# Delta heads: the next head's decays move from the solver to the scan, one difference and one weight split ahead of the masks, the taps behind the residuals

## Chip, core and metric

One core of a Trainium2 chip runs the whole kernel. The metric is the device time of one execution in microseconds; several executions are timed and their median is taken. The timed executions of the kernel before are 2096.05, 2089.41 and 2095.82.

## What is computed

One transformer block in fp32 (`D_MODEL` 1024, 512 tokens and 256 context tokens): a gated FFN, a mixer (grouped attention beside a gated delta rule in both directions), and a second FFN. The change touches only the delta rule, 8 heads of width 128. Cut to what matters:

```python
def _delta_rule(q, k, v, beta, g, s0):          # per head, in chunks
    gcum = jnp.cumsum(gc, axis=-1)
    decay = jnp.exp(jnp.where(lower_incl, gcum[..., :, None] - gcum[..., None, :], -jnp.inf))
    kb = kc * bc[..., None]
    l_mat = jnp.where(strict, jnp.einsum('nbhid,nbhjd->nbhij', kb, kc) * decay, 0.0)
    rhs = jnp.concatenate([vc * bc[..., None], kb * jnp.exp(gcum)[..., None]], axis=-1)
    sol = lax.linalg.triangular_solve(l_mat, rhs, left_side=True, lower=True, unit_diagonal=True)
    u, w = sol[..., :dv], sol[..., dv:]
    intra = jnp.where(lower_incl, jnp.einsum('nbhid,nbhjd->nbhij', qc, kc) * decay, 0.0)
    def step(s, xs):
        v_new = u_c - jnp.einsum('bhcd,bhde->bhce', w_c, s)
        o = jnp.einsum('bhcd,bhde->bhce', q_d, s) + jnp.einsum('bhij,bhje->bhie', a_c, v_new)
        s = s * d_c[..., None, None] + jnp.einsum('bhcd,bhce->bhde', k_d, v_new)
```

q, k and v of a head come from a GEMM, a convolution of three taps, silu, and (q, k) an l2 norm. The kernel uses chunks of 128 tokens, `NCH` = 6 of them, which gives the same result.

## The kernel before, in words

Each engine runs its own program (blocks `scalar` with `a`, `vector` with `v`, `gpsimd` with `g`, `tensor` with `pe`, `sync` with `sp`), in the order written out by hand, and semaphores join them: `then_inc` on an instruction, `wait_ge` ahead of one. An engine works in order, so what is queued behind a waiting instruction waits too.

**Weights.** The weights come in blocks of 128x1024. SP loads a block into the ring `raw`; `split(b)` on ScalarE rounds it into `w_hi` (L411), `split(b)` on VectorE subtracts (`w_lo`, L812, a tensor operation on two SBUF tensors), and the GEMM of the block waits for `w_split`. `step(b)` on VectorE is the split of the block two further on. A head has four blocks: 0 to 3 are q, k, v and the output gate z; `Blk(B_DN, h, 4)` to `(h, 6)` are those of the next head.

**A delta head** (`dn_head`, a loop over heads 0 to 6, and head 7 written out as the final one) has these parts on TensorE: sums of squares, GEMM of block 3, products k k and k q, transposes, three zero matmuls, the GEMM of the next head's block 4 (in all but the final head), transposes into `ps` (L1668), the **solver**, a **scan** over 6 chunks, and the rest of the next head's GEMMs, of which pieces (`fill`) lie in the scan.

**The solver** inverts a triangular matrix by levels: 18 steps `i`, three groups in each of six levels. In a step VectorE masks (`masked(i)`, L1226, reads PSUM and a mask in SBUF), TensorE multiplies (`mid(i)`, then `grow(i-1)`), ScalarE copies (L721). GpSimd makes each level's `d_s` (L370), and between them `d_qd` (L381), `d_kd` (L388) and `d_l` (L393). All of GpSimd's products here are tensor operations on two SBUF tensors.

**The scan** has for each chunk `t`: TensorE `from_keys(t)`, VectorE `residual(t)` (two of L1264), TensorE `solve(t)`, ScalarE `d_vn` (two of L730), TensorE `to_state(t)`, VectorE `new_state(t)` (two of L1274, at t = 0 of L1272).

**The decays.** For both directions d, VectorE takes the difference of cumulated gates (`decay_diff`, L1182, from the row table `g_row` that a GpSimd-issued DMA loads) into `d_q[:, 1]`, clips it (`decay_min`, L1187, into `d_t`), and makes the max with a mask (`decay_max`, L1190, into `d_r`). ScalarE exponentiates (`decay` L661, `decay_out` L665). `d_t[:, 0]` is multiplied by beta on VectorE, `d_t[:, 1]` on GpSimd (L363). In the kernel before these are made for the next head inside the solver, between masks.

On VectorE the order around the change is: norms of q and k, `step(b[2])`, products that lead to `d_l`, the off-mask products (L1218, L1221), `attn_mul` twice (L1232), `tables_next` (a copy of `hn`, L1153), the 18 masks with `step(b[3])` and the decays between them, three masks L1253, `step` of block 4, and the scan with one convolution tap (L1171, L1174) in each of the first three chunks.

Of the kernel before, what the change touches and what calls it, by code (L numbers as in the profile page):

```python
# [23 lines left out]
P = 128  # L24
# [5 lines left out]
NCH = NC_CTX + NC_X  # L30
# [55 lines left out]
def build(nc, W, WMOD, XT, VEC, CONV, CA, CB, OUT, XS, GR):  # L86
    ctx = ExitStack()
    with ctx:
# [316 lines left out]
        def _(a):  # L405
# [251 lines left out]
                split(b.ahead(2))  # L657

            def decay(h, d):
                a.wait_ge(s("d_mn"), h * 4 + (2 * d + 1))  # L660
                a.activation(d_t[:, d], d_t[:, d], ACT.Exp).then_inc(s("d_e1"), 1)  # L661

            def decay_out(h, d):
                a.wait_ge(s("d_mn"), h * 4 + (2 * d + 2))
                a.activation(d_r[:, d, 0:NC_X], d_r[:, d, 0:NC_X], ACT.Exp, scale=-1.0).then_inc(s("d_e2"), 1)  # L665

            def activate(h, ahead):
# [13 lines left out]
            def dn_head(h, final):  # L681
                b = [Blk(B_DN, h, j) for j in range(4)]
                take(b[2])
                a.wait_ge(s("d_ss"), h + 1)
                a.activation(d_rs[:, 0:SEQ], ps[:, 4, :], ACT.Ln, bias=eps_q, scale=float(DH))
                a.activation(d_rs[:, SEQ:SEQ + CTX], ps[:, 5, 0:CTX], ACT.Ln, bias=eps)
                a.activation(d_rs[:, SEQ + CTX:], ps[:, 6, :], ACT.Ln, bias=eps).then_inc(s("d_ln"), 1)
                a.wait_ge(s("d_ln"), h * 2 + 1)
                a.activation(d_rs[:], d_rs[:], ACT.Exp, scale=-0.5).then_inc(s("d_rstd"), 1)
                split(b[2].ahead(2))  # L690
                a.wait_ge(s("d_row"), h * 16 + 16)
                for d in range(2):
                    a.activation(d_qd[:, d], g_row[:, d, NC_CTX:], ACT.Exp).then_inc(s("d_qe"), 1)  # L693
                a.preload_act_table_set(SILU_SET)  # L694
                a.wait_ge(s("conv"), h * 3 + 3)
                a.activation(d_c[:, 2, :], d_c[:, 2, :], ACT.Silu).then_inc(s("d_silu"), 1)  # L696
                a.wait_ge(s("gemm_done"), b[3].n + 1)
                a.activation(d_z[:], bank(b[3], 1), ACT.Silu).then_inc(psum_read[b[3].pair], 1)
                a.preload_act_table_set(LOG_SET)  # L699

                a.wait_ge(s("d_tok"), h * 2 + 1)
                a.activation(d_ktok[:, 0:3].rearrange("p c n -> p (c n)"), ps[:, 2, 0:384], ACT.Copy)
                a.activation(d_ktok[:, 3:6].rearrange("p c n -> p (c n)"), ps[:, 7, 0:384], ACT.Copy).then_inc(s("d_tokc"), 1)
                split(b[3].ahead(2))
                a.wait_ge(s("d_tok"), h * 2 + 2)
                a.activation(d_vtok[:].rearrange("p (b c) n -> p b (c n)", b=2), ps[:, 0:2, 0:384], ACT.Copy).then_inc(s("d_tokc"), 1)
                a.wait_ge(s("t_open"), h + 1)
                for gr in range(3):
                    a.wait_ge(s("t_set"), h * 3 + gr + 1)
                    a.activation(ps[:, TRB[gr], 0:2 * P], d_q[:, 1, 2 * gr:2 * gr + 2].rearrange("p c n -> p (c n)"),  # L710
                                 ACT.Copy).then_inc(s("t_ps"), 1)
                if not final:
                    take_first(Blk(B_DN, h, 4))
                def scaled(c):
                    x = a.activation(d_l[:, 1, c], d_vtok[:, c], ACT.Identity, scale=hc[:, G_BETA + 6 + c:G_BETA + 7 + c])
                    if c == NCH - 1:
                        x.then_inc(s("d_vb"), 1)
                a.wait_ge(s("d_tokc"), h * 2 + 2)
                for i in range(18):
                    a.wait_ge(s("sv_q"), h * 18 + (i + 1))  # L720
                    a.activation(d_q[:, 0, 2 * (i % 3):2 * (i % 3) + 2].rearrange("p c n -> p (c n)"), ps[:, 2 + i % 2, 0:2 * P],  # L721
                                 ACT.Copy).then_inc(s("sv_qc"), 1)
                    if i < NCH:
                        scaled(i)
                    if not final and i in (6, 7, 12, 13):
                        (decay if i % 2 == 0 else decay_out)(h + 1, (i - 6) // 6)
                for t in range(NCH):
                    for d in range(2):
                        a.wait_ge(s("sc_t"), h * 12 + 2 * t + d + 1)
                        a.activation(d_vn[:, d, t % 2], ps[:, 4 + d, P:2 * P], ACT.Copy, scale=-1.0 if t else 1.0).then_inc(s("sc_n"), 1)  # L730
                if not final:
                    take(Blk(B_DN, h, 5))
                a.wait_ge(s("od_copy"), h + 1)
                a.activation(d_os[:], d_o[:], ACT.Square).then_inc(s("od_sq"), 1)
                if final:
                    round_attention(0, 6)
                    step(Blk(B_MERGE, 0, 0))
                else:
                    activate(h + 1, Blk(B_DN, h, 7))
                a.wait_ge(s("od_ss"), h + 1)  # L740
                a.activation(d_os[:], ps[:, 7, :], ACT.Ln, bias=eps, scale=1.0 / DH).then_inc(s("d_ln"), 1)
                a.wait_ge(s("d_ln"), h * 2 + 2)
                a.activation(d_os[:], d_os[:], ACT.Exp, scale=-0.5).then_inc(s("od_rstd"), 1)
# [3 lines left out]
            a.activation(d_up[:, CTX + 3:T + 3], bank(first[0], 1), ACT.Copy).then_inc(psum_read[first[0].pair], 1)  # L747
            split(first[0].ahead(2))
            for d in range(2):
                decay(0, d)  # L750
                decay_out(0, d)
            take(first[1])
            activate(0, first[1].ahead(2))
            with a.Fori(0, H - 1, 1) as h:
# [53 lines left out]
        def _(v):  # L808
# [368 lines left out]
            def decay_diff(h, d):  # L1177
                if d == 0:
                    v.wait_ge(s("d_row"), h * 16 + 16)
                else:  # L1180
                    v.wait_ge(s("d_mn"), h * 4 + 2)
                v.tensor_tensor(d_q[:, 1], hn[:, G_GC + 6 * d:G_GC + 6 * d + 6].unsqueeze(2).to_broadcast([P, NCH, P]),  # L1182
                                g_row[:, d], ALU.subtract).then_inc(s("d_diff"), 1)

            def decay_min(h, d):
                v.wait_ge(s("d_diff"), h * 2 + (d + 1))
                v.tensor_scalar(d_t[:, d], d_q[:, 1], 0.0, None, ALU.min).then_inc(s("d_mn"), 1)  # L1187

            def decay_max(d):
                v.scalar_tensor_tensor(d_r[:, d, 0:NC_X], d_q[:, 1, NC_CTX:], 0.0,  # L1190
                                       no_tri[:, d, :].unsqueeze(1).to_broadcast([P, NC_X, P]), ALU.max, ALU.add)\
                 .then_inc(s("d_mn"), 1)

            def dn_head(h, final):
                b = [Blk(B_DN, h, j) for j in range(4)]
# [2 lines left out]
                v.tensor_tensor(d_c[:, 1, 0:CTX], d_c[:, 1, 0:CTX], d_rs[:, SEQ:SEQ + CTX], ALU.mult)  # L1198
                v.tensor_tensor(d_c[:, 1, CTX + 2:], d_c[:, 1, CTX + 2:], d_rs[:, SEQ + CTX:], ALU.mult).then_inc(s("d_qk"), 1)
                v.tensor_tensor(d_c[:, 0, CTX + 2:], d_c[:, 0, CTX + 2:], d_rs[:, 0:SEQ], ALU.mult).then_inc(s("d_qk"), 1)  # L1200
                step(b[2])
                v.wait_ge(s("d_e1"), h * 2 + 1)
                v.tensor_tensor(d_t[:, 0], d_t[:, 0], bc(hc[:, G_BETA:G_BETA + 6]), ALU.mult).then_inc(s("d_eb0"), 1)

# [7 lines left out]
                v.tensor_tensor(d_l[:, 0].rearrange("p (b c) n -> p b (c n)", b=2),  # L1212
                                d_t[:, 0].rearrange("p (b c) n -> p b (c n)", b=2), ps[:, 4:6, 0:384], ALU.mult)\
                 .then_inc(s("d_l"), 1)
                v.wait_ge(s("d_l"), h + 1)
                for gr in range(3):
                    x = d_q[:, 1, 2 * gr:2 * gr + 2]
# [18 lines left out]
                attn_mul(1)  # L1236
                if not final:
                    tables_next(h + 1)
                for i in range(18):
                    masked(i)  # L1240
                    if i == 7:
                        step(b[3])
                    if final:
                        continue
                    if i in (2, 9):
                        decay_diff(h + 1, i // 9)
                    if i in (4, 11):
                        decay_min(h + 1, i // 11)
                    if i in (5, 12):
                        decay_max(i // 12)  # L1250
                for gr in range(3):
                    v.wait_ge(s("sv_t"), h * 21 + 18 + gr + 1)
                    v.tensor_tensor(d_w[:, gr].rearrange("p (d c) n -> p d c n", d=2),  # L1253
# [2 lines left out]
                if not final:  # L1256
                    v.wait_ge(psum_read[Blk(B_DN, h, 4).pair], Blk(B_DN, h, 4).turn + 2)
                    step(Blk(B_DN, h, 4))
                    v.wait_ge(s("d_qd"), h * 2 + 2)
                def residual(t):  # L1260
                    for d in range(2):
                        c = ORDER[d][t]
# [14 lines left out]
                for t in range(NCH):  # L1277
                    if t:
                        residual(t)
                    if t < NCH - 1:  # L1280
                        new_state(t)
                    if t < 3 and not final:
                        conv_tap(h + 1, 0, t)
                if not final:
                    v.wait_ge(s("sc_v"), h * 10 + 10)
                    tables(h + 1)
# [17 lines left out]
            step(Blk(B_DN, 0, 0))  # L1304
            for d in range(2):
                decay_diff(0, d)
                decay_min(0, d)
                decay_max(d)
            conv(0, 0, Blk(B_DN, 0, 0))
            conv(0, 1, Blk(B_DN, 0, 1))  # L1310
            step(Blk(B_DN, 0, 1))
# [589 lines left out]
```

## Time and profile before

| what | value |
|---|---|
| median of the three runs | 2095.82 us |
| the profiled execution | 2089.0 us |
| its span in the profile | 2087.3 us |
| TensorE busy | 2005.8 us (96%) |
| VectorE / ScalarE / GpSimd busy | 1126.4 / 797.7 / 225.4 us |
| mean granted TensorE clock | 0.985 of full speed |
| one delta head (transposes of head 0 at 913.36, of head 6 at 1353.79) | 73.4 us |

A row of the timeline has: start in us from the span's start, duration in us, engine, line and operation, output and inputs with their shapes, the count of merged instructions, and in brackets the idle time of the engine before it and what ended it.
### The profile page before, as it was taken

The numbers are of one execution on the slowest core, as the hardware profiler recorded it, in microseconds if no ns is written. First come the engines' busy times: TensorE is split into PE (matmuls) and PEld (weight loads), VectorE is DVE, ScalarE is ACT, GpSimd is POOL, SyncE is SP. The second block draws the span as 40 slices with busy tenths as digits, with TensorE's granted clock in tenths as the row PEclk, the third lists the DMA queues.
The fourth block names the chain that finished last, engine by engine and source line by source line (L and its number), as shares of the span: only waits on it lengthen the run. The fifth ranks groups of instructions, "written<-read, shape, count | busy, mean of one in ns | idle before, by whom it ended". The sixth has DMA issues, their size and how long they took to land.

```text
span 2087.3 us, 31229 instructions
## 1 busy us (share of the span) xinstructions
PE 2005.8 (96%) x11329; PEld 1714.1 (82%) x11329; DVE 1126.4 (54%) x2027; ACT 797.7 (38%) x1291; POOL 225.4 (11%) x211
## 2 busy tenths in 40 slices
PE   8999999999996999999999999999999979999996
PEld 4788888888884779888988888898888858888885
DVE  2677655555456655476676667666533353233335
ACT  4322222111236555465456536544422352223122
POOL 0000000000000210041342144133000000000000
PEclk9999999999998999999999999999999999999998
DMA  8233333333221330011011001100222413222322
GB/s 310 88 119 118 119 123 122 128 121 123 79 81 68 116 92 1 11 46 46 30 45 45 33 33 45 45 29 22 71 98 93 141 40 102 100 97 95 101 91 80
DMA packets 49035, 174.73 MB, mean 84 GB/s; under 512 B 6724, under 2 KB 6852, under 8 KB 48720
## 3 DMA queue, kind: packets, MB, share of 16 engines
q1 hardware_dynamic: 37632, 129.95, 18.4%
q0 software_dynamic: 11344, 43.97, 6.3%
q8 instruction: 40, 0.66, 0.1%
q14 instruction: 19, 0.16, 0.0%
HBM read 167.03 MB, written 4.24 MB: 82 GB/s over the span
## 4 chain that ended last, share of the span: by engine, by line
PE 86%; issue 5%; ACT 4%; DVE 4%; POOL 1%; DMA 0%; ACTq 0%; DVEq 0%; SPq 0%; POOLq 0%
PE ps L1370 79%; PE ps L1374 4%; PE ps L1608 1%; DVE d_w L1226 1%; ACT w_hi L411 1%; DVE X L894 1%; DVE n_y L886 1%; PE ps L1737 1%; POOL d_s L370 1%; DVE w_lo L812 0%; ACT L699 0%; ACT L694 0%; ACT d_qd L693 0%; ACT d_c L696 0%; DMA X<-XT 0%
## 5 line engine op out<-in xcount | busy, mean ns | idle before, releaser
L1370 PE MATMUL ps<-h_hi,w_hi 128*128 128x512 f32 (+1 forms) x1712 | 547.4, 369 | 16.7 <-DVE h_lo L869 10.9
L411 ACT ACTIVATE w_hi<-raw 128x1024 fp32r<-128x1024 f32 x221 | 233.8, 1058 | 794.5 <-PE ps L1370 794.5
L1370 PE MATMUL ps<-h_lo,w_hi 128*128 128x512 f32 (+1 forms) x1712 | 536.3, 360 | 0.0
L1370 PE MATMUL ps<-h_hi,w_lo 128*128 128x512 f32 (+1 forms) x1712 | 528.6, 358 | 0.0
L812 DVE TENSOR_TENSOR w_lo<-raw,w_hi 128x1024 fp32r<-128x1024 f32 x221 | 272.2, 1232 | 437.8 <-ACT w_hi L411 437.6
L1370 PEld LDWEIGHTS ps<-h_hi,w_hi 128*128 128x128 f32 x1712 | 318.8, 189 | 72.5 <-issue 22.9
L1370 PEld LDWEIGHTS ps<-h_lo,w_hi 128*128 128x128 f32 x1712 | 323.4, 189 | 49.1 <-issue 3.4
L1370 PEld LDWEIGHTS ps<-h_hi,w_lo 128*128 128x128 f32 x1712 | 323.6, 189 | 48.5
L1370 PE MATMUL ps<-g_hi,w_hi 128*128 128x512 f32 (+1 forms) x528 | 158.4, 355 | 0.0
L1370 PE MATMUL ps<-g_lo,w_hi 128*128 128x512 f32 (+1 forms) x528 | 157.9, 354 | 0.0
L1370 PE MATMUL ps<-g_hi,w_lo 128*128 128x512 f32 (+1 forms) x528 | 157.9, 354 | 0.0
L1226 DVE TENSOR_TENSOR d_w<-ps,cb 128x512 f32<-128x512 f32 x144 | 97.0, 686 | 64.9 <-PE ps L1374 44.4
L928 DVE TENSOR_TENSOR gt<-sg,ps 128x256 f32<-128x256 f32 (+1 forms) x66 | 37.5, 596 | 136.6 <-PE ps L1370 136.6
L1370 PEld LDWEIGHTS ps<-g_hi,w_lo 128*128 128x128 f32 x528 | 99.3, 188 | 14.1
L1370 PEld LDWEIGHTS ps<-g_lo,w_hi 128*128 128x128 f32 x528 | 99.3, 188 | 14.0
L1374 PE MATMUL ps<-d_q,d_w 128*128 128x128 f32 x576 | 110.1, 280 | 0.2
L1370 PEld LDWEIGHTS ps<-g_hi,w_hi 128*128 128x128 f32 x528 | 98.9, 188 | 13.8
L370 POOL TENSOR_TENSOR d_s<-d_l,cb 128x768 f32<-128x768 f32 x48 | 92.0, 1922 | 121.8 <-DVE d_q L1221 83.7
L1370 PE MATMUL ps<-d_w,d_s 128*128 128x128 f32 x576 | 92.9, 286 | 8.3 <-DVE d_w L1226 6.7
L721 ACT ACTIVATE d_q<-ps 128x256 f32<-128x256 f32 x144 | 55.2, 383 | 108.9 <-PE ps L1370 108.8
L1374 PE MATMUL ps<-d_w,d_q 128*128 128x128 f32 x480 | 93.8, 278 | 0.0
L831 DVE SCALAR_TENSOR_TENSOR m_part<-w_mod,silc,m_part 128x128 f32<-128x128 f32 x336 | 90.4, 343 | 0.0
(264 smaller groups left out, 2687.3 us busy)
## 6 DMA issues: line engine op xcount, KB each, us to landing
raw<-W SPq DMA_DIRECT2D x221, 512.0 KB, 3.4
w_mod<-WMOD POOLq DMA_DIRECT2D x56, 512.0 KB, 3.7
w_mod<-WMOD SPq DMA_DIRECT2D x16, 512.0 KB, 14.2
g_row<-g_rows POOLq DMA_DIRECT2D x8, 768.0 KB, 6.2
X<-XT SPq DMA_DIRECT2D x4, 768.0 KB, 7.4
a_sw<-i_n POOLq DMA_DIRECT2D x40, 64.0 KB, 1.9
x_spill<-X POOLq DMA_DIRECT2D x1, 2048.0 KB, 7.7
X<-x_spill POOLq DMA_DIRECT2D x1, 2048.0 KB, 8.4
```

Source lines behind the costliest of these rows:

```text
L370: g.tensor_tensor(d_s[lv % 2][:], d_l[:, 0], off_mask[:, lv, :].unsqueeze(1).to_broadcast([P, NCH, P]), ALU.mult).then_inc(s("lvl"), 1)
L411: a.activation(w_hi[:, b.pair], raw[:, b.raw], ACT.Copy).then_inc(s("w_hi"), 1)
L721: a.activation(d_q[:, 0, 2 * (i % 3):2 * (i % 3) + 2].rearrange("p c n -> p (c n)"), ps[:, 2 + i % 2, 0:2 * P], ACT.Copy).then_inc(s("sv_q ...
L812: v.tensor_tensor(w_lo[:, b.pair], raw[:, b.raw], w_hi[:, b.pair].bitcast(F32), ALU.subtract)\
L831: x = v.scalar_tensor_tensor(acc, w_mod[:, slot, k, :], silc[:, k, c:c + 1], acc, ALU.mult, ALU.add)
L886: v.tensor_tensor(n_y[:, k % 4, lo:T], cols(Y, Y2, p, k, lo, T), n_rs[:, lo:T], ALU.mult).then_inc(s("yn"), 1)
L894: last = v.scalar_tensor_tensor(x, n_y[:, k % 4, l:h_], drv[:, 2 * p + 1, k, sg_:sg_ + 1], x, ALU.mult, ALU.add)
L928: last = v.tensor_tensor(gt[:, l:h_], sg[:, l:h_], bank(blk, sg_), ALU.mult)
L1226: v.tensor_tensor(d_w[:, gr], ps[:, TRB[gr], :].rearrange("p (c n) -> p c n", c=4), tri_mask[:, lv - 1, :].unsqueeze(1).to_broadcast([P, 4 ...
L1370: return pe.matmul(out, lhsT, rhs, start=start, stop=stop)
L1374: return pe.matmul(out, lhsT, rhs, start=False, stop=True, skip_group_check=True)
L1608: last = pe.transpose(ps[:, c // 3, P * (c % 3):P * (c % 3) + P], a_p[:, i % 2, P * c:P * c + P], ident)
```

## The change

Six things move, nothing is added or left out of the computation:

- the differences are written into `d_t`, no more into `d_q[:, 1]`, and the clip works in place behind the max (`decay_clip`), with a wait between the two;
- difference 0 of the next head goes from behind mask 2 to ahead of mask 0, difference 1 from behind mask 9 to behind mask 2;
- the clips and maxes go from the solver to the scan: direction 0 ahead of `new_state(0)`, direction 1 behind `residual(1)`; ScalarE's exponentials go to the chunks 1 to 4 of the scan;
- `step(b[3])` goes from behind mask 7 to ahead of mask 0 (in the final head too);
- `step(b[2])` goes behind the product `d_l`;
- the taps go from behind `new_state` of chunks 0 to 2 to behind `residual` of chunks 2 to 4.

```diff
@@ scalar @@
             def decay(h, d):
+                a.wait_ge(s("d_mn"), h * 4 + (2 * d + 2))
+                a.activation(d_t[:, d], d_t[:, d], ACT.Exp).then_inc(s("d_e1"), 1)
+
+            def decay_out(h, d):
                 a.wait_ge(s("d_mn"), h * 4 + (2 * d + 1))
-                a.activation(d_t[:, d], d_t[:, d], ACT.Exp).then_inc(s("d_e1"), 1)
-
-            def decay_out(h, d):
-                a.wait_ge(s("d_mn"), h * 4 + (2 * d + 2))
                 a.activation(d_r[:, d, 0:NC_X], d_r[:, d, 0:NC_X], ACT.Exp, scale=-1.0).then_inc(s("d_e2"), 1)
...
-                    if not final and i in (6, 7, 12, 13):
-                        (decay if i % 2 == 0 else decay_out)(h + 1, (i - 6) // 6)
                 for t in range(NCH):
...
+                    if not final and t in (1, 2, 3, 4):
+                        (decay if t % 2 else decay_out)(h + 1, (t - 1) // 2)
@@ vector @@
             def decay_diff(h, d):
                 if d == 0:
                     v.wait_ge(s("d_row"), h * 16 + 16)
-                else:
-                    v.wait_ge(s("d_mn"), h * 4 + 2)
-                v.tensor_tensor(d_q[:, 1], hn[:, G_GC + 6 * d:G_GC + 6 * d + 6].unsqueeze(2).to_broadcast([P, NCH, P]),
+                v.tensor_tensor(d_t[:, d], hn[:, G_GC + 6 * d:G_GC + 6 * d + 6].unsqueeze(2).to_broadcast([P, NCH, P]),
                                 g_row[:, d], ALU.subtract).then_inc(s("d_diff"), 1)
 
-            def decay_min(h, d):
+            def decay_clip(h, d):
                 v.wait_ge(s("d_diff"), h * 2 + (d + 1))
-                v.tensor_scalar(d_t[:, d], d_q[:, 1], 0.0, None, ALU.min).then_inc(s("d_mn"), 1)
-
-            def decay_max(d):
-                v.scalar_tensor_tensor(d_r[:, d, 0:NC_X], d_q[:, 1, NC_CTX:], 0.0,
+                v.scalar_tensor_tensor(d_r[:, d, 0:NC_X], d_t[:, d, NC_CTX:], 0.0,
                                        no_tri[:, d, :].unsqueeze(1).to_broadcast([P, NC_X, P]), ALU.max, ALU.add)\
                  .then_inc(s("d_mn"), 1)
+                v.wait_ge(s("d_mn"), h * 4 + (2 * d + 1))
+                v.tensor_scalar(d_t[:, d], d_t[:, d], 0.0, None, ALU.min).then_inc(s("d_mn"), 1)
...
-                step(b[2])
                 v.wait_ge(s("d_e1"), h * 2 + 1)
...
+                step(b[2])
                 v.wait_ge(s("d_l"), h + 1)
...
                     tables_next(h + 1)
+                    decay_diff(h + 1, 0)
+                step(b[3])
                 for i in range(18):
                     masked(i)
-                    if i == 7:
-                        step(b[3])
-                    if final:
-                        continue
-                    if i in (2, 9):
-                        decay_diff(h + 1, i // 9)
-                    if i in (4, 11):
-                        decay_min(h + 1, i // 11)
-                    if i in (5, 12):
-                        decay_max(i // 12)
+                    if i == 2 and not final:
+                        decay_diff(h + 1, 1)
...
                     step(Blk(B_DN, h, 4))
-                    v.wait_ge(s("d_qd"), h * 2 + 2)
+                    decay_clip(h + 1, 0)
...
                         residual(t)
+                    if not final and t == 1:
+                        decay_clip(h + 1, 1)
+                    if not final and t in (2, 3, 4):
+                        if t == 2:
+                            v.wait_ge(s("d_qd"), h * 2 + 2)
+                        conv_tap(h + 1, 0, t - 2)
                     if t < NCH - 1:
                         new_state(t)
-                    if t < 3 and not final:
-                        conv_tap(h + 1, 0, t)
```

## Rows read from the trace of the kernel before

**Rows 1.** Page, the chain of work that ended last, by engine.
```profile
PE 86%; issue 5%; ACT 4%; DVE 4%; POOL 1%; DMA 0%; ACTq 0%; DVEq 0%; SPq 0%; POOLq 0%
```

**Rows 2.** TensorE's waits, whole span: us in total, times, longest.
```profile
PE ps L1370 <- ACT d_ktok L703: 7.4, 8, 0.9
```

**Rows 3.** Timeline of TensorE, head 2: transposes, `mid(0)`, and steps 2, 6, 15.
```profile
1060.16 0.82 PE L1668 MATMUL ps<-ca,d_q 128*128 128x128 f32 x6
1061.33 1.31 PE L1370 MATMUL ps<-d_w,d_s 128*128 128x128 f32 x8 [0.35 <-DVE d_w L1226]
...
1063.51 0.61 PE L1370 MATMUL ps<-d_w,d_s 128*128 128x128 f32 x4
...
1068.87 0.61 PE L1370 MATMUL ps<-d_w,d_s 128*128 128x128 f32 x4
...
1082.48 0.61 PE L1370 MATMUL ps<-d_w,d_s 128*128 128x128 f32 x4
```

**Rows 4.** Timeline of VectorE in the same solver, the work between masks.
```profile
1069.67 1.44 DVE L812 TENSOR_TENSOR w_lo<-raw,w_hi 128x1024 fp32r<-128x1024 f32 x1
...
1075.36 1.46 DVE L1187 TENSOR_SCALAR d_t<-d_q 128x768 f32<-128x768 f32 x1
...
1077.34 1.70 DVE L1190 SCALAR_TENSOR_TENSOR d_r<-d_q,no_tri 128x512 f32<-128x512 f32 x1
```

**Rows 5.** Timeline of VectorE before the loop, while GpSimd is idle.
```profile
882.32 0.56 DVE L1187 TENSOR_SCALAR d_t<-d_q 128x768 f32<-128x768 f32 x1
882.80 0.69 DVE L1190 SCALAR_TENSOR_TENSOR d_r<-d_q,no_tri 128x512 f32<-128x512 f32 x1
```

**Rows 6.** Timeline of GpSimd in head 2.
```profile
1055.92 3.64 POOL L370 TENSOR_TENSOR d_s<-d_l,cb 128x768 f32<-128x768 f32 x2 [5.18 <-DVE d_q L1221]
1059.52 1.08 POOL L381 TENSOR_TENSOR d_qd<-d_qd,d_c 128x512 f32<-128x512 f32 x1
...
1069.99 2.46 POOL L388 TENSOR_TENSOR d_kd<-d_ktok,hc 128x768 f32<-128x768 f32 x1
...
1076.59 1.90 POOL L370 TENSOR_TENSOR d_s<-d_l,cb 128x768 f32<-128x768 f32 x1 [0.18 <-PE ps L1370]
```

**Rows 7.** Timeline of VectorE ahead of the masks, head 2.
```profile
1056.94 0.87 DVE L1153 COPY hn<-gall 128x69 f32 x1
1060.58 1.89 DVE L1226 TENSOR_TENSOR d_w<-ps,cb 128x512 f32<-128x512 f32 x3 [2.77 <-PE ps L1668]
```

**Rows 8.** Timeline of VectorE from the end of the solver into the scan.
```profile
1087.31 1.22 DVE L812 TENSOR_TENSOR w_lo<-raw,w_hi 128x1024 fp32r<-128x1024 f32 x1
...
1092.94 0.60 DVE L1274 SCALAR_TENSOR_TENSOR d_st<-d_st,hc,ps 128x128 f32<-128x128 f32 x2 [1.39 <-PE ps L1370]
```

**Rows 9.** The row table's load: GpSimd's timeline, and DMA issues of the page.
```profile
1050.14 0.59 POOL L333 DMA_DIRECT2D g_row<-g_rows  x1 [41.73 <-ACT d_qd L693]
...
g_row<-g_rows POOLq DMA_DIRECT2D x8, 768.0 KB, 6.2
```

**Rows 10.** Timeline of TensorE in the scan: `from_keys` and `to_state` of chunks 3, 4.
```profile
1096.48 0.66 PE L1370 MATMUL ps<-d_st,d_c 128*128 128x128 f32 x4
...
1098.60 0.61 PE L1370 MATMUL ps<-d_vn,d_kd 128*128 128x128 f32 x4
...
1099.97 0.60 PE L1370 MATMUL ps<-d_st,d_c 128*128 128x128 f32 x4
...
1101.83 0.61 PE L1370 MATMUL ps<-d_vn,d_kd 128*128 128x128 f32 x4
```

**Rows 11.** Timeline of TensorE in the final head, `mid(0)`.
```profile
1424.80 2.08 PE L1370 MATMUL ps<-d_w,d_s 128*128 128x128 f32 x8 [0.51 <-POOL d_s L370]
```

**Rows 12.** TensorE's timeline ahead of the delta heads, and windows there (PEclk third from right).
```profile
871.10 0.65 PE L1370 MATMUL ps<-h_hi,w_hi 128*128 128x512 f32 x1 [2.22 <-issue]
...
871.00:872.00 1.00, 0.90 (x3) 0.74 (x4) 0.05 (x1) 0.00 (x0) 0.00 (x0) 0.61 0.00 0
...
874.00:875.00 1.00, 1.00 (x4) 0.77 (x4) 0.00 (x0) 0.00 (x0) 0.00 (x0) 0.68 0.08 16
```

More of the change, by code:

```diff
@@ L659, in decay @@
             def decay(h, d):
-                a.wait_ge(s("d_mn"), h * 4 + (2 * d + 1))
+                a.wait_ge(s("d_mn"), h * 4 + (2 * d + 2))
                 a.activation(d_t[:, d], d_t[:, d], ACT.Exp).then_inc(s("d_e1"), 1)
             def decay_out(h, d):
-                a.wait_ge(s("d_mn"), h * 4 + (2 * d + 2))
+                a.wait_ge(s("d_mn"), h * 4 + (2 * d + 1))
                 a.activation(d_r[:, d, 0:NC_X], d_r[:, d, 0:NC_X], ACT.Exp, scale=-1.0).then_inc(s("d_e2"), 1)
@@ L749, in _ @@
             for d in range(2):
+                decay_out(0, d)
                 decay(0, d)
-                decay_out(0, d)
             take(first[1])
@@ L1306, in _ @@
                 decay_diff(0, d)
-                decay_min(0, d)
-                decay_max(d)
+                decay_clip(0, d)
             conv(0, 0, Blk(B_DN, 0, 0))
```

## Prediction

> **What bounds the kernel now.** I read the chain of waits first, because it tells which engine the end time is made of: TensorE's instructions are 86% of it, VectorE and ScalarE 4% each [rows 1]. So an edit on VectorE counts only where TensorE waits for it. The change touches only the delta stage, eight heads of about 73.4 us; seven of them prepare a next head. I therefore read one of these heads (head 2, counted from 0) on TensorE's timeline, looking for places where it isn't back to back, then VectorE's and GpSimd's timelines at those places. In the list of TensorE's waits the regular entries of this stage are the 0.9 us before the zero matmuls, which wait for ScalarE's `d_ktok` [rows 2] and which the change doesn't touch, and the waits for masks.
>
> In the solver `mid` starts every 1.34 us when nothing disturbs it: step 2 at 1063.51, step 6 at 1068.87, so 5.36 for four steps. Step 15 starts at 1082.48; thirteen clean steps would be 17.42, it took 18.97 [rows 3]. **1.55 us per head** are thus lost to VectorE's other work between masks. The rows show whose: `w_lo` takes 1.44, the clip `d_t` 1.46 and the max `d_r` 1.70 [rows 4], while outside GpSimd's work the clip takes 0.56, the max 0.69, and `w_lo` 1.22 [rows 5, 8].
>
> **Why they stretch.** GpSimd's level product started at 1076.59 and ended at 1078.49; the max, issued at 1077.34, ended at 1079.04, that is 0.69 after about 1078.35 [rows 4, 6]. It didn't run at half speed, it waited until the product was all but over and then took its normal time. The other way round, `w_lo` held until 1071.11 and GpSimd's `d_kd` product, started at 1069.99, took 2.46 and ended at 1072.45: 1.47 of it lie behind `w_lo` [rows 4, 6]. The wait is over some 0.13 us before the holder's recorded end. Masks, which read PSUM and one SBUF tensor, are 0.69 throughout. So two-SBUF-tensor operations, copies and SBUF clips of VectorE exclude GpSimd's products, and these exclude them. The Trainium skill (SBUF — State Buffer, section "Who interferes with whom") states the same as a rule, that the one that issues first has the shared ports for its whole instruction; by that rule, which speaks against this change at the solver's entry, the trace agrees, with the 1.70 and 2.46 above.
>
> **The change, part by part** (times of before, head 2).
>
> *Decays out of the solver.* Clips, maxes, their exponentials and `w_lo` leave it; one difference stays behind mask 2, where mask 3 has slack and GpSimd is idle. GpSimd's products then fit: a level needs 1.82 (half of 3.64), a `d_kd` product 1.47, against 4.02 us of TensorE for three steps. Next late is TensorE itself at 1.34. Gain 1.55, taken as **-1.53** (the final head, with only `w_lo` inside, shows about the same clean pace). Bounds -1.2 (some loss stays) to -1.55.
>
> *`step(b[2])` moved behind `d_l`.* It runs 1052.2 to 1053.4. TensorE needs this block after the zero matmuls at 1054.38, which wait for ScalarE anyway [rows 2]. The off-mask products start when they did. The cover is 0.9 us; without it, it would cost up to 1.2. SP's weight load behind it starts some 3 us later, and the other block's 9 us earlier; no wait for a weight load shows in this stage. **0**.
>
> *First difference and `step(b[3])` ahead of mask 0.* Free VectorE time is there: 2.77 us before the masks [rows 7] against 0.95 + 1.22. But GpSimd works through it: two level products from 1055.92 to 1059.56, then the `d_qd` product from 1059.52 [rows 6]. Already the tiny copy of `hn` has 0.87 there, because it waits for the first product's end [rows 7]. By the rows, the difference comes ready at about 1057.87, after the second level product has started, waits until 1059.43 and ends at 1060.38. Now the `d_qd` product has waited since 1059.52, and `w_lo` comes ready at 1060.31. The copy of `hn` got between two products that GpSimd issued back to back; by symmetry GpSimd gets between the difference and `w_lo`. Then the product holds until 1061.20, `w_lo` ends at 1062.42, and mask 0 starts at 1062.35 instead of 1060.58 [rows 7]: **+1.77**. If `w_lo` keeps the ports, mask 0 starts at 1061.45: +0.87. Bounds 0 to 2.0. The row table lands 6.2 us after its issue at 1050.14 [rows 9], at 1056.4, so the difference doesn't wait for it; margin 1.5 us. Queued behind the difference are `w_lo` and all masks, and TensorE waits for the masks.
>
> *Clips and maxes in the scan.* A max and a clip take 0.69 + 0.56 + about 0.04 for the wait between them. The first pair goes behind `w_lo`, ahead of `new_state(0)`, the second between `residual(1)` and `new_state(1)`. VectorE is idle at the second place for 1.39 us [rows 8], at the first for as long, and GpSimd has nothing to do. They fit with 0.1 us left. If the wait is the longer 0.18, it costs 0.05. **0**, bound +0.4 a head.
>
> *Taps moved behind the residuals.* A tap now stands between `new_state` and `residual`. From `from_keys(3)` to `to_state(3)` TensorE takes 1098.60 - 1096.48 = 2.12, with a tap in the way; at step 4, without one, 1101.83 - 99.97 = 1.86 [rows 10]. That is 0.26 gained at step 3, and about half that at step 2, where a filler keeps TensorE busy. Taps of 0.48 and 0.75 go into gaps of about 1.25 us. **-0.35**, bounds 0 to -0.5. ScalarE's exponentials go into its gaps between the copies `d_vn`, which are over twice as long as the longest of them. GpSimd's beta product follows the third of them; it could hold the last tap back 0.2 us, within that gap, and residuals read PSUM and one SBUF tensor.
>
> *Final head.* Here masks aren't held by a GEMM. `mid(0)` starts at 1424.80, when GpSimd's first level product has ended [rows 11]. `w_lo` now stands before mask 0 and waits for that product, to about 1424.6: it ends 1.22 later, at 1425.8, mask 0 at 1426.45, and `mid(0)` starts at about 1426.5. +1.7, less 0.3 at its old place: **+1.4**, bounds 0.5 to 2.5. Head 0's decays before the loop lie under GEMMs: 0.
>
> Sum without the clock: 7 x (1.77 - 1.53 - 0.35) + 1.4 = **+0.6 us**.
>
> **TensorE's clock.** With mask 0 at 1062.35, TensorE is idle from the transposes' end at 1060.98 [rows 3] to about 1063.1, 2.1 us instead of 0.35. In this trace an idle stretch of 2.2 us after dense work (it ended at 871.10) was followed by granted clock 0.50, that is 1.2 GHz, from 871.2 to 874.7 [rows 12]; the longer stretches fell too. The regular idles of 0.9 us [rows 2] never did. 2.1 is nearest to 2.2, just under it; I take five heads of seven. Each 3.4 us at half the clock lose 1.7 us where TensorE is the bound, as in the solver: 5 x 1.7 = +8.5; bounds 0 and 7 x 1.7 = +12. Sum 0.6 + 8.5 = **+9.1**, taken as +9.5, since the final head's slow stretch may grow too.
>
> The profiled execution took 2089.0 (span 2087.3), 6.8 under the median of 2095.82; the runs lie at two levels, 2089.4 and 2096. I take the middle, 2092.5: 2092.5 + 9.5 = **2102**.
>
> **Rivals.**
> 1. *GpSimd gets in and the clock holds* (2.1 us idle isn't enough, or only in one or two heads): +0.6 to +4. Against it the 2.2 us row; for it that no row has 2.1. About 2094.
> 2. *`w_lo` keeps the ports*: TensorE is idle 1.2 us, the clock holds, 7 x (0.87 - 1.88) + 1.4 = -5.7, about 2087. For it: VectorE starts an instruction 0.07 us before the last one's recorded end, about when the ports come free. It decides if that start comes before GpSimd gets hold.
> 3. *Nothing is in the way at the entry* (the difference wins over the second level product, and `w_lo` follows it): mask 0 as before, -1.88 x 7 + 1.4 = -11.7, about 2081 to 2084. Against it: the copy's 0.87.
> 4. *The change doesn't do what it says in the scan*: a max and clip that don't fit delay `new_state` by up to 0.4 a head, +3 on any case.
>
> **How the numbers follow.** Forecast (GpSimd in between, clock falls in four heads or more) 0.43; rival 1 0.17; rival 2 0.20; rival 3 0.12; rival 4 and others 0.08. The upper end is 2096 + 0.6 + 12 + 1 = 2110; the lower one takes in rival 2 from the lower level and most of rival 3: 2083. Both signs hold much of the chance: the forecast's own range is 2096 to 2110. 0.3% is 6.3 us, about what a measurement of this kernel can tell from no change. Slower by more: the forecast nearly whole, 0.44 with rival 4. Within: rival 1, most of rival 2, rest, 0.36. Faster: rival 3 and the edge of rival 2, 0.20.
>
> **What would show it.** In the profile after: `w_lo` ahead of mask 0 at 2.1 us or more, with the `d_qd` product between it and the difference; the difference itself at 2.5 instead of 0.95; TensorE idle 2.1 us before `mid(0)`; granted clock 0.5 in the solver's first steps; `mid` at 1.34 us from step 3 on; clip and max at 0.56 and 0.69 in the scan; `new_state` idle for 0.1 instead of 1.4. If `w_lo` shows 1.22, rival 2 or 3 holds. The prediction is wrong if the clock stays at 1.00 in the solver, or if the difference shows 0.95.

## The result, and the profile after

| | before | changed |
|---|---|---|
| median of 20 runs each | 2097.2 us | 2105.06 us |
| ratio | | 1.004, 95% interval 1.0026 to 1.0055 |
| span of the profiled execution | 2087.3 us | 2103.7 us |
| from the zero matmuls of head 0 to those of the final head | 513.92 us | 521.15 us |

The change costs 8 us, 0.4%. The medians take in all 20 executions, the ratio leaves out three slow ones (3371.73 and 5823.14 before, 2385.55 changed).

The spans of the two profiled executions differ by 16.4, but 8.5 of these lie before the first delta head: the zero matmuls of head 0 start at 907.49 before and 915.97 after. The executions of every kernel here come at two levels some 10 us apart (before 2088 to 2090 and 2096 to 2100, changed 2094 to 2098 and 2104 to 2108), and the profiled ones fell on different ones; at like level the change costs some 7 us. The levels aren't made by the change: a second profile of the changed kernel (last experiment) is of the lower level, and in it the same zero matmuls start at 905.78. The difference arises in the first FFN, where TensorE runs 887 matmuls between 200 and 350 us in that profile and in the one of before, and 871 in the first profile of the changed kernel, with a granted clock of 1.00 in all three. Why isn't known. So below I compare single heads and stretches, which don't depend on it.

In the page's chain of the changed kernel TensorE has 90% instead of 86 and ScalarE 1% instead of 4 (before: [rows 1]). Newly named in it are VectorE's operations ahead of the solver (L1215, L1229, L1153), each with a share that rounds to 0%:

```profile
PE 90%; DVE 4%; issue 3%; ACT 1%; DMA 0%; DVEq 0%; POOL 0%; SPq 0%; ACTq 0%
PE ps L1364 82%; PE ps L1368 7%; PE ps L1602 1%; DVE X L894 1%; DVE n_y L886 1%; PE ps L1731 1%; DVE w_lo L812 0%; DVE d_q L1215 0%; DVE d_at L1229 0%; ACT w_hi L411 0%; DVE hn L1153 0%; DVE d_w L1223 0%; DMA ca<-CA 0%; ACT n_t L472 0%; ACT n_rs L443 0%
```

TensorE's waits over the whole span (us in total, times, longest): the wait for a mask is now one of 2.1 us in each looping head and 2.3 in the final one. The wait for `d_ktok` is what it was in [rows 2].

```profile
PE ps L1364 <- DVE d_w L1223: 16.8, 8, 2.3
PE ps L1364 <- ACT d_ktok L703: 7.5, 8, 0.9
```

VectorE's timeline of the changed kernel at the entry of the solver in head 5, which answers to [rows 7], and GpSimd's, which answers to [rows 6]:

```profile
1290.44 0.88 DVE L1153 COPY hn<-gall 128x69 f32 x1
1291.45 2.44 DVE L1180 TENSOR_TENSOR d_t<-hn,g_row 128x768 f32<-128x768 f32 x1
1293.81 2.11 DVE L812 TENSOR_TENSOR w_lo<-raw,w_hi 128x1024 fp32r<-128x1024 f32 x1
1295.84 1.87 DVE L1223 TENSOR_TENSOR d_w<-ps,cb 128x512 f32<-128x512 f32 x3
```

```profile
1289.42 3.65 POOL L370 TENSOR_TENSOR d_s<-d_l,cb 128x768 f32<-128x768 f32 x2 [5.19 <-DVE d_q L1218]
1293.04 1.80 POOL L381 TENSOR_TENSOR d_qd<-d_qd,d_c 128x512 f32<-128x512 f32 x1
```

The difference ends at 1293.89, 2.44 after it was ready, and 0.95 of that is work. The `d_qd` product, waiting since 1293.04, goes next (it takes 1.80, and 1.08 in [rows 6]), and `w_lo` ends at 1295.92, which is its own 1.2 us behind 1294.7, just before the recorded end of the product at 1294.84. The order is level product, difference, `d_qd` product, `w_lo`, mask.

TensorE's timeline at that place in head 4 and, as its last row, head 5, which answers to [rows 3], and windows of both behind it (PEclk third from right):

```profile
1220.50 0.82 PE L1662 MATMUL ps<-ca,d_q 128*128 128x128 f32 x6
1223.40 1.31 PE L1364 MATMUL ps<-d_w,d_s 128*128 128x128 f32 x8 [2.08 <-DVE d_w L1223]
...
1225.58 0.61 PE L1364 MATMUL ps<-d_w,d_s 128*128 128x128 f32 x4
...
1243.00 0.61 PE L1364 MATMUL ps<-d_w,d_s 128*128 128x128 f32 x4
...
1296.58 1.82 PE L1364 MATMUL ps<-d_w,d_s 128*128 128x128 f32 x8 [2.08 <-DVE d_w L1223]
```

```profile
1224.00:1226.00 2.00, 2.00 (x17) 1.94 (x17) 1.63 (x3) 1.27 (x4) 0.00 (x0) 1.00 0.73 244
1298.00:1300.00 2.00, 2.00 (x11) 2.00 (x11) 0.58 (x1) 0.84 (x3) 0.00 (x0) 0.50 0.42 170
```

Both heads idle 2.08 us. In head 4 the clock stays at 1.00 and from step 2 to step 15 it takes 1243.00 - 1225.58 = 17.42, as thirteen clean steps should; in head 5 the clock falls to 0.50 for 3.4 us, and 11 matmuls run in two microseconds instead of 17. The clock fell in six of the seven looping heads. From one head's zero matmuls to the next it took, in order:

| | head 0 | 1 | 2 | 3 | 4 | 5 | 6 |
|---|---|---|---|---|---|---|---|
| before | 73.49 | 73.40 | 73.39 | 73.40 | 73.41 | 73.43 | 73.40 |
| changed | 74.46 | 74.67 | 74.80 | 74.80 | 73.17 | 74.57 | 74.68 |

The scan of the changed kernel, VectorE's timeline in head 4, where the first pair of max and clip stands ahead of `new_state(0)` and the second behind `residual(1)`; it answers to [rows 8]:

```profile
1247.83 1.22 DVE L812 TENSOR_TENSOR w_lo<-raw,w_hi 128x1024 fp32r<-128x1024 f32 x1
1248.96 0.68 DVE L1185 SCALAR_TENSOR_TENSOR d_r<-d_t,no_tri 128x512 f32<-128x512 f32 x1
1249.68 0.56 DVE L1189 TENSOR_SCALAR d_t<-d_t 128x768 f32<-128x768 f32 x1
1250.44 0.51 DVE L1263 COPY d_st<-ps 128x128 f32<-128x128 f32 x2 [0.20 <-PE ps L1364]
...
1253.46 0.60 DVE L1265 SCALAR_TENSOR_TENSOR d_st<-d_st,hc,ps 128x128 f32<-128x128 f32 x2 [0.19 <-PE ps L1364]
```

The second pair, left out above, has the same 0.68 and 0.56. Both leave 0.2 us of idle time before the state: they cost nothing.

### The profile page after: what moved, and what is told of

It reads as the page before. It is cut to its first block, busy times and chain, and to the rows that moved or that the text cites. A ratio compares the mean times of both kernels' runs of the same rounds, so it can differ in the third digit from the quotient of the medians.

```text
span 2103.7 us, 31229 instructions
## 1 busy us (share of the span) xinstructions
PE 2014.0 (96%) x11329; PEld 1719.8 (82%) x11329; DVE 1130.5 (54%) x2027; ACT 798.2 (38%) x1291; POOL 214.7 (10%) x211
## 4 chain that ended last, share of the span: by engine, by line
PE 90%; DVE 4%; issue 3%; ACT 1%; DMA 0%; DVEq 0%; POOL 0%; SPq 0%; ACTq 0%
PE ps L1364 82%; PE ps L1368 7%; PE ps L1602 1%; DVE X L894 1%; DVE n_y L886 1%; PE ps L1731 1%; DVE w_lo L812 0%; DVE d_q L1215 0%; DVE d_at L1229 0%; ACT w_hi L411 0%; DVE hn L1153 0%; DVE d_w L1223 0%; DMA ca<-CA 0%; ACT n_t L472 0%; ACT n_rs L443 0%
## 5 line engine op out<-in xcount | busy, mean ns | idle before, releaser
L812 DVE TENSOR_TENSOR w_lo<-raw,w_hi 128x1024 fp32r<-128x1024 f32 x221 | 277.2, 1255 | 443.3 <-ACT w_hi L411 443.1
L1364 PEld LDWEIGHTS ps<-d_w,d_s 128*128 128x128 f32 x576 | 80.6, 203 | 19.7 <-DVE d_w L1223 16.2
```

Of the source, the lines that this page charges most:

```text
L812: v.tensor_tensor(w_lo[:, b.pair], raw[:, b.raw], w_hi[:, b.pair].bitcast(F32), ALU.subtract)\
L1364: return pe.matmul(out, lhsT, rhs, start=start, stop=stop)
```

## Experiments

Theory: VectorE's operations on two SBUF tensors and GpSimd's products exclude each other. The `d_qd` product gets between the difference and `w_lo`, mask 0 comes 1.75 us late, and the idle time of TensorE lets its clock fall. Rivals: VectorE has simply too much to do ahead of the masks; the loss is made in the scan; the slow stretches have another cause. In each fence of an experiment the stretch is that of head 6, unless it says otherwise.

**Both differences back inside the solver** (against the changed kernel):

```diff
                     tables_next(h + 1)
-                    decay_diff(h + 1, 0)
                 step(b[3])
                 for i in range(18):
                     masked(i)
-                    if i == 2 and not final:
-                        decay_diff(h + 1, 1)
+                    if i in (2, 5) and not final:
+                        decay_diff(h + 1, i // 5)
```

> The changed kernel, with both differences of the next head back inside the solver (behind masks 2 and 5); the split w_lo of block 5 stays ahead of mask 0. Exclusion theory: w_lo comes ready while the second level product holds the ports, waits until its end and takes about 2.8 in all, mask 0 starts within 0.1 us of where it did in the kernel before, TensorE idles 0.35 to 0.45 us ahead of mid(0), the clock stays at 1.00 in the seven looping heads, and such a head takes 73.40 - 1.55 - 0.40 = 71.45 us. Whole: 12 us under the kernel before (the final head still pays 1.4 to 1.8). Rival, too much VectorE work ahead of the masks whatever GpSimd does: only the 0.95 of the difference is won, mask 0 is still 0.8 late, a head takes 72.2. Rival, the loss is made in the scan: heads stay at 73.2 and more.

Measured: every looping head 71.43 to 71.46 us, idle time ahead of `mid(0)` 0.34 to 0.35, no fall of the clock in them. Ratio to the kernel before 0.993 (0.9905 to 0.9955), median 2076.6 against 2088.55. VectorE's timeline at the entry, then GpSimd's:

```profile
1350.86 2.71 DVE L812 TENSOR_TENSOR w_lo<-raw,w_hi 128x1024 fp32r<-128x1024 f32 x1
1353.51 1.89 DVE L1223 TENSOR_TENSOR d_w<-ps,cb 128x512 f32<-128x512 f32 x3
```

```profile
1352.45 2.07 POOL L381 TENSOR_TENSOR d_qd<-d_qd,d_c 128x512 f32<-128x512 f32 x1
```

`w_lo` is longer than in the changed kernel (2.71), and yet the masks are on time, because it waits for one product only and has its wait under the GEMM; now the `d_qd` product is the one that waits. Taking away 0.95 us of work gave 1.73 (73.17, head 4 of the changed kernel, against 71.44). Too much work by itself would have given 0.95.

**`w_lo` back inside the solver** (behind mask 7, in the final head too), the difference stays ahead of mask 0:

```diff
                     decay_diff(h + 1, 0)
-                step(b[3])
                 for i in range(18):
                     masked(i)
+                    if i == 7:
+                        step(b[3])
```

> The changed kernel, with w_lo of block 5 back behind mask 7; the first difference stays ahead of mask 0. Exclusion theory: the difference still takes 2.4 (it waits for the second level product) but ends before the transposes do, mask 0 is on time, no fall of the clock, and w_lo costs some 0.3 us at step 7: a head of 71.75 us. Rival, too much VectorE work: 1.22 won of 1.77, mask 0 0.5 late, a head of 72.3.

Measured: looping heads 71.76 to 71.82, idle 0.35, no fall in them. VectorE's timeline:

```profile
1354.53 2.44 DVE L1180 TENSOR_TENSOR d_t<-hn,g_row 128x768 f32<-128x768 f32 x1
1357.17 1.89 DVE L1223 TENSOR_TENSOR d_w<-ps,cb 128x512 f32<-128x512 f32 x3 [0.21 <-PE ps L1663]
...
1366.27 1.44 DVE L812 TENSOR_TENSOR w_lo<-raw,w_hi 128x1024 fp32r<-128x1024 f32 x1
```

The difference alone fits, with 0.21 us left, though it takes 2.44. So either of the two can stand ahead of mask 0; not both. With the split among the masks a head takes 71.77 - 71.44 = 0.33 more than with the differences there.

**GpSimd's `d_qd` products one level later**, VectorE's program untouched:

```diff
-                    if lv in (3, 4):
-                        d = lv - 3
+                    if lv in (4, 5):
+                        d = lv - 4
```

> The changed kernel, VectorE's order untouched, but GpSimd makes its two d_qd products one level later each (ahead of levels 4 and 5), so that it has nothing to do behind the second level product. Exclusion theory: the difference still takes 2.4, w_lo right behind it takes 1.22 instead of 2.11, mask 0 comes 0.9 us earlier, TensorE idles about 1.2 instead of 2.08, the clock stays at 1.00, a head takes 73.2 - 0.9 = 72.3 us. Rival, VectorE's own work or the wait for w_hi holds w_lo: it stays at 2.1, and idle, clock and head stay as they are.

Measured: looping heads 72.29 to 72.31, idle 1.16 to 1.20, no fall in them. VectorE's timeline, then TensorE's:

```profile
1355.51 2.43 DVE L1180 TENSOR_TENSOR d_t<-hn,g_row 128x768 f32<-128x768 f32 x1
1357.87 1.21 DVE L812 TENSOR_TENSOR w_lo<-raw,w_hi 128x1024 fp32r<-128x1024 f32 x1
```

```profile
1359.73 0.97 PE L1364 MATMUL ps<-d_w,d_s 128*128 128x128 f32 x5 [1.20 <-DVE d_w L1223]
```

With the product gone from behind the difference, `w_lo` takes 1.21 instead of 2.11 at the same place in the same order. That is the exclusion shown by itself, and its price: 0.9 us a head. With 1.2 us of idle time instead of 2.08 the clock held in all seven heads, so the longer stretch and with it the falls hang on this hand-over too.

**Work for TensorE in the idle time**, everything else as in the changed kernel. The added products are thrown away:

```diff
+                if not final:
+                    pe.wait_ge(s("d_am"), h * 2 + 2)
+                    for k in range(7):
+                        mm(ps[:, 6, :], h_hi[:, k, CTX:CTX + P], h_hi[:, k, CTX:T])
+
                 def mid(i):
```

> The changed kernel plus seven 128x512 matmuls of h_hi by h_hi on TensorE between the transposes and mid(0), in the looping heads; their sum goes into a PSUM bank that nobody reads before it is started anew. They fill 1.6 of the 2.08 us of idle time and leave the masks where they are. Clock theory: granted clock stays at 1.00 in all seven heads, each takes 73.2 us instead of 74.8 in six of them, and the whole is 9 to 10 us faster than the changed kernel, 1 us within the kernel before. Rival, the slow stretches have another cause, or cost nothing: six or seven of the heads still fall, or heads stay at 74.8 with the clock at 1.00.

Measured: looping heads 73.19 to 73.25, idle 0.48 to 0.50, clock 1.00 in all seven; ratio to the kernel before 1.0014 (0.9993 to 1.0036), with 5 of its 10 runs at the upper level and 3 of the 14 of before. Timeline of TensorE and a window behind it:

```profile
1354.09 1.85 PE L1364 MATMUL ps<-h_hi 128*128 128x512 f32 x7
1356.44 1.31 PE L1364 MATMUL ps<-d_w,d_s 128*128 128x128 f32 x8 [0.50 <-DVE d_w L1223]
```

```profile
1358.00:1360.00 2.00, 2.00 (x21) 2.00 (x20) 1.14 (x2) 1.13 (x4) 0.69 (x1) 1.00 0.36 147
```

The masks are exactly as late as in the changed kernel (`w_lo` 2.11), and all heads take what head 4 took there. Useless work made these heads faster. From the zero matmuls of head 0 to those of the final head it takes 512.45 us, against 521.15 in the changed kernel. So the whole excess of the other heads, 8.7 us in sum, is the clock, and without the idle stretch it doesn't fall.

**The end of the reasoning, as a kernel:** the first experiment, with `w_lo` of the final head back behind mask 7.

```diff
                     tables_next(h + 1)
-                    decay_diff(h + 1, 0)
-                step(b[3])
+                    step(b[3])
                 for i in range(18):
                     masked(i)
-                    if i == 2 and not final:
-                        decay_diff(h + 1, 1)
+                    if i == 7 and final:
+                        step(b[3])
+                    if i in (2, 5) and not final:
+                        decay_diff(h + 1, i // 5)
```

> The kernel of e1_diff_inside, with w_lo of the final head back behind mask 7, where the kernel before has it. Exclusion theory: looping heads stay at 71.44 us; in the final head w_lo no longer holds up the second level product and mask 0, so mid(0) there starts 3.4 us after the zero matmuls instead of 5.2, and the whole is 13 to 14 us (0.65%) under the kernel before and 1.4 us under e1. Rival: the slow clock of the final head eats this, and it is level with e1.

Measured: looping heads 71.46 to 71.50; in the final head `mid(0)` starts 3.40 after the zero matmuls, instead of 5.16 in the first experiment. From the final head's zero matmuls to the end it takes 665.8 us against 667.4, 1.6 less. How much of that is the edit a single pair doesn't say: the slow stretch of the clock in the final head is 6.8 us long in the first experiment and 3.4 here. Over all nine traces of this document the four kernels with `w_lo` behind mask 7 take 664.7 to 665.9 there, and the five profiles with it ahead of mask 0 take 666.6 to 667.4, 1.7 more in the mean. Ratio to the kernel before 0.9948 (0.9928 to 0.9969), median 2083.79 against 2089.06. 7 of its 12 runs were at the upper of the two levels, but only 6 of 17 of the kernel before; at like level it is some 13 us faster (2073 to 2076 against 2086 to 2089). So the gain is 0.52% as measured and 13/2087 = 0.62% at like level. The totals can't tell it from the first experiment, and the forecast of 13 to 14 us holds at like level alone. VectorE's timeline in the final head:

```profile
1422.44 1.88 DVE L1223 TENSOR_TENSOR d_w<-ps,cb 128x512 f32<-128x512 f32 x3
```

**The taps alone**, on the kernel before:

```diff
-                    v.wait_ge(s("d_qd"), h * 2 + 2)
                 def residual(t):
...
                         residual(t)
+                    if not final and t in (2, 3, 4):
+                        if t == 2:
+                            v.wait_ge(s("d_qd"), h * 2 + 2)
+                        conv_tap(h + 1, 0, t - 2)
                     if t < NCH - 1:
                         new_state(t)
-                    if t < 3 and not final:
-                        conv_tap(h + 1, 0, t)
```

> The kernel before with one edit: the three taps go from behind new_state of chunks 0 to 2 to behind residual of chunks 2 to 4. The scan term by itself: 0.35 to 0.40 us less per looping head, 73.0 instead of 73.4, from_keys(3) to to_state(3) in 1.86 instead of 2.12. Rival, the scan's gain in the changed kernel comes from the clips or from TensorE's pieces: heads stay at 73.4.

Measured (one run): looping heads 72.99 to 73.04, 0.40 less than before. TensorE's timeline of head 2, `from_keys(3)` and `to_state(3)`: 1097.36 - 1095.48 = 1.88, against 2.12 in [rows 10].

```profile
1095.48 0.66 PE L1371 MATMUL ps<-d_st,d_c 128*128 128x128 f32 x4
...
1097.36 0.61 PE L1371 MATMUL ps<-d_vn,d_kd 128*128 128x128 f32 x4
```

**The changed kernel once more**, unedited:

> The changed kernel once more, unedited. The idle ahead of mid(0) should be 2.08 us in every looping head again, since it follows from the instruction order. Which heads fall to 1.2 GHz may differ: by the forecast five to seven; each head with a fall 74.5 to 74.8 us, each without 73.2. If the fall were fixed by the program, the same head (the fifth) would stay at 1.00 again.

Measured: idle 2.08 to 2.10 in all looping heads. Heads 1, 3, 4, 5 and 6 fell (74.56 to 74.84), heads 0 and 2 did not (73.22). In the first profile only head 4 did not. TensorE's timeline and windows of heads 2 and 3:

```profile
1062.53 1.31 PE L1364 MATMUL ps<-d_w,d_s 128*128 128x128 f32 x8 [2.10 <-DVE d_w L1223]
...
1135.74 1.61 PE L1364 MATMUL ps<-d_w,d_s 128*128 128x128 f32 x7 [2.10 <-DVE d_w L1223]
```

```profile
1065.00:1067.00 2.00, 2.00 (x20) 2.00 (x20) 1.29 (x2) 0.98 (x4) 1.60 (x1) 1.00 0.00 0
1136.00:1138.00 2.00, 2.00 (x12) 2.00 (x12) 1.74 (x3) 1.08 (x4) 0.00 (x0) 0.51 0.81 254
```

The same idle stretch of 2.10 us was followed by a fall in one head and by none in another. The length of the idle time alone doesn't settle it; the program doesn't either, since the heads differ between two executions of it. The row on which the forecast of the falls rested, 2.22 us of idle time ahead of the delta heads [rows 12], is no rule either. Here the same stretch is followed by no fall; TensorE's timeline, and two windows behind it:

```profile
871.00 0.47 PE L1364 MATMUL ps<-h_hi,w_hi 128*128 128x512 f32 x1 [2.22 <-issue]
...
871.00:872.00 1.00, 1.00 (x4) 0.83 (x5) 0.00 (x0) 0.00 (x0) 0.00 (x0) 1.00 0.00 0
874.00:875.00 1.00, 1.00 (x6) 0.81 (x6) 0.00 (x0) 0.00 (x0) 0.00 (x0) 1.00 0.00 0
```

What the traces do show is an order. In the first profile the clock falls 0.3, 0.9, 1.3 and 1.6 us behind the start of `mid(0)` in heads 0 to 3, not at all in head 4, and 0.4 and 0.9 behind it in heads 5 and 6. In the second it is none, 1.6, none, 0.3, 0.9, 1.3, 1.5. So the fall isn't tied to the end of the idle stretch: it comes later from head to head, and each time behind a head with 1.6 comes one without a fall. The moment at which the stretch comes thus seems to decide along with its length. No run moved the stretch alone, so this is a regularity of two traces and not a shown cause.

## Why the prediction was right

The forecast was 2102, of a range of 2083 to 2110, slower being the likeliest; measured were 2105.06 and a ratio of 1.004. Step by step, per looping head:

| step | predicted | measured | from |
|---|---|---|---|
| decays and `w_lo` out of the solver | -1.53 | -1.55 | steps 2 to 15 in 17.42 against 18.97 |
| entry of the solver | +1.77 | +1.75 | `mid(0)` 8.70 behind the zero matmuls against 6.95 |
| `step(b[2])` behind `d_l` | 0 | 0 | waits for `d_ktok` 7.5 in sum against 7.4 |
| clips and maxes in the scan | 0 | 0 | idle 0.2 left before both states |
| taps | -0.35 | -0.40 | taps alone on the kernel before |
| sum without a fall | -0.11 | -0.2 | 73.17 against 73.40 |
| a fall of the clock | 1.7, five of seven | 1.3 to 1.6, six of seven | heads of 74.46 to 74.80 against 73.17 |
| all seven heads | +7.7 | +7.2 | 521.15 against 513.92 |

- *Entry.* The argument by symmetry held: as VectorE's copy of `hn` had got between two products of GpSimd, GpSimd's product got between two operations of VectorE. Rival 2 (`w_lo` keeps the ports) and rival 3 (the difference wins) would have shown 1.22 and 0.95; the rows show 2.11 and 2.44. The third experiment priced the point at which they part at 0.9 us a head.
- *Clock.* The step rested on one row, the 2.2 us of idle time in [rows 12]. It held in six heads of seven in one execution and five in another, but the row itself didn't hold in the second execution (last experiment), and "five of seven" was read off a nearness of 2.1 to 2.2, not derived: that the count came out is luck in part. The size was too high, 1.3 to 1.6 instead of 1.7. It was smallest, 1.3, where the fall came 0.3 us behind the start of `mid(0)`, and 1.6 where it came 1.3 or 1.6 behind it, so the first steps of the solver lose less by the slow clock than the later ones. Rival 1, that the clock holds, is what head 4 showed in the first execution and heads 0 and 2 in the second, but not as a rule.
- *Final head.* I had +1.4. `mid(0)` is 1.77 later than before (5.17 behind the zero matmuls instead of 3.39), but from there to the end of the kernel it cost 0.7 in this profile (666.6 against 665.9), and 1.2 to 1.4 in the three other kernels that have this edit; by the means over all nine traces it is 1.7 (fifth experiment). TensorE's clock is slow in the final head in all of them, for 6.8 us in every profile with this edit, and for 3.4 us in three of the four without it. The falls there stand behind shorter idle stretches than those of the looping heads, as already in the kernel before, where the clock falls at 1424.2. TensorE's timeline of before in the final head, ahead of [rows 11]:

```profile
1421.41 0.49 PE L1370 MATMUL ps<-no_tri,zeros 128*128 128x256 bf16 x3 [0.93 <-ACT d_ktok L703]
1423.33 0.95 PE L1668 MATMUL ps<-ca,d_q 128*128 128x128 f32 x6 [1.43 <-ACT ps L710]
```

The prediction had looked at single stretches alone and not at two of 0.93 and 1.43 us with half a microsecond of work between them.
- *The base.* I had taken the middle of two levels, 2092.5, while the median of before turned out 2097.2; on it the sum of +9.5 would have given 2107. So the forecast came within 3 us of the measured time because a base 4.7 too low and a sum 1.6 too high offset each other. The measured difference of 7.9 is -1.5 for the heads without a fall (512.45 of the filler kernel against 513.92), +8.7 for the clock (521.15 against 512.45) and +0.7 for the final head. The forecast had -0.8, +8.5, +1.4 and 0.4 for a longer slow stretch in the final head. The clock's sum thus came out though its two factors didn't: six falls of some 1.5 instead of five of 1.7.

## What to carry to other kernels

Before a VectorE operation is put into a gap of its timeline, look at what GpSimd does in that gap: operations on two SBUF tensors and SBUF copies and clips wait for a product's end and let the next product in between them, so two that fit by their durations (0.95 + 1.22 into 2.77 us) can take 4.5. With GpSimd's products waiting, a gap that took one such operation didn't take two; with GpSimd idle, in the scan, a gap of 1.4 us took two. And the price of an idle stretch of TensorE isn't its length alone: here 1.75 us of lateness was paid back by the rest of the change, and what made the kernel slower were the falls of the clock behind it.

## What was not expected of the hardware

- Seven matmuls whose results nobody reads, 1.6 us of TensorE's time in each head, make the heads of the changed kernel faster, from up to 74.8 to 73.2 us a head, by keeping the clock at 1.00.
- The same idle stretch (2.04 to 2.10 us) is followed by a fall to 1.2 GHz in 11 of 14 heads over two executions, and by none in the other three.
- The row table's load lands 4.5 us after its issue in the changed kernel (median of 8), 6.2 in the kernel before ([rows 9]). Its issue stands in the same place of GpSimd's program; VectorE's order behind it differs. Nothing waits for it in either, and no run was made for it, so the cause stays open. The pages of the experiments narrow it: 4.2 to 4.5 in every kernel built on the changed one, whatever stands at the solver's entry, and 6.0 in the kernel before with the taps moved, so neither the entry nor the taps make it. The page's row of the changed kernel:

```profile
g_row<-g_rows POOLq DMA_DIRECT2D x8, 768.0 KB, 4.5
```
